# A hybrid RG-LRU / gated DeltaNet / attention backbone in fp32: four moves at the entry of the delta net

## What is computed

```python
q, k, v = jnp.split(jax.nn.silu(dw_conv(qkv, dn_cw)), [...], axis=-1)
q = l2_normalize(q.reshape(bsz, L, DN_HEADS, DN_DK)) * (DN_DK ** -0.5)
k = l2_normalize(k.reshape(bsz, L, DN_HEADS, DN_DK))
...
gcum = jnp.cumsum(to_chunks(g[..., None])[..., 0], axis=-1)
decay = jnp.exp(jnp.where(causal, gcum[..., :, None] - gcum[..., None, :], -jnp.inf))
m = jnp.where(strict, jnp.einsum('nbhid,nbhjd->nbhij', k_beta, kc) * decay, 0.0)
sol = lax.linalg.triangular_solve(eye + m, rhs, left_side=True, lower=True, unit_diagonal=True)
...
q_dec = qc * jnp.exp(gcum)[..., None]
```

## Time and profile before

| | |
|---|---|
| median of 3 runs | 1340.19 us |
| lowest, highest | 1338.09, 1348.91 us |
| the profiled execution, its own time | 1343.36 us |
| its span | 1341.6 us |
| TensorE busy | 1304.7 us (97%) |
| VectorE, ScalarE, GpSimd busy | 859.0 (64%), 681.5 (51%), 290.8 us (22%) |
| chain that ended last | TensorE 77%, VectorE 10%, ScalarE 5%, issue 3%, GpSimd 2%, DMA 1% |
| mean granted TensorE clock | 0.991 of full speed |

### The profile page before, as it was taken

One profiled execution on the slowest core, in us unless ns is written; L12 is line 12 of the kernel. 1 busy time (PEld: TensorE's weight loads), 2 busy tenths in 40 slices (PEclk: granted clock), 3 DMA queues, 4 the chain that ended last, 5 costly groups with the idle time before them and its releaser, 6 DMA issues.

```text
span 1341.6 us, 27229 instructions
## 1 busy us (share of the span) xinstructions
PE 1304.7 (97%) x10946; PEld 1226.9 (91%) x10946; DVE 859.0 (64%) x1271; ACT 681.5 (51%) x1098; POOL 290.8 (22%) x368
## 2 busy tenths in 40 slices
PE   6999999999799999999999999999999999999998
PEld 4899999997688888999999999999999988999998
DVE  4754789995457666533677656666736666875663
ACT  4458888866555554322534212343236665664553
POOL 3000223412587897513000000000130000200002
PEclk8999999999899999999999999999999999999999
DMA  9722323244231111123466566565423321556662
GB/s 325 209 80 81 94 79 95 80 114 151 98 111 33 49 48 33 64 95 110 146 202 196 181 193 195 183 197 178 129 95 126 97 69 32 182 173 220 190 201 80
DMA packets 138926, 174.90 MB, mean 130 GB/s; under 512 B 11025, under 2 KB 121873, under 8 KB 138561
## 3 DMA queue, kind: packets, MB, share of 16 engines
q1 hardware_dynamic: 137312, 168.94, 39.9%
q10 hardware_dynamic: 896, 4.23, 0.9%
q0 software_dynamic: 608, 0.19, 0.1%
HBM read 172.25 MB, written 1.08 MB: 129 GB/s over the span
## 4 chain that ended last, share of the span: by engine, by line
PE 77%; DVE 10%; ACT 5%; issue 3%; POOL 2%; DMA 1%; SPq 0%; ACTq 0%; DVEq 0%; POOLq 0%
PE bank L2728 54%; PE bank L2736 4%; DVE w_lo L1778 3%; DVE qkv L1864 2%; PE bank L3132 2%; PE bank L3141 2%; ACT w_hi L951 1%; PE bank L2654 1%; POOL qkv L806 1%; PE bank L3087 1%; PE bank L3408 1%; PE bank L3431 1%; DMA first_w<-in_w_mod 1%; PE bank L3006 1%; PE bank L3074 1%
## 5 line engine op out<-in xcount | busy, mean ns | idle before, releaser
L1778 DVE TENSOR_TENSOR w_lo<-raw,w_hi 128x1024 fp32r<-128x1024 f32 x212 | 264.2, 1247 | 297.1 <-ACT w_hi L951 296.6
L951 ACT ACTIVATE w_hi<-raw 128x1024 fp32r<-128x1024 f32 x212 | 223.9, 1057 | 379.9 <-PE bank L2728 371.8
L2728 PE MATMUL bank<-h_hi,w_hi 128*128 128x256 f32 x1472 | 299.4, 282 | 5.4 <-DVE w_lo L1778 2.9
L2728 PE MATMUL bank<-h_hi,w_lo 128*128 128x256 f32 x1472 | 293.7, 278 | 0.0
L2728 PE MATMUL bank<-h_lo,w_hi 128*128 128x256 f32 x1472 | 288.3, 278 | 0.0
L2728 PEld LDWEIGHTS bank<-h_hi,w_hi 128*128 128x128 f32 x1472 | 225.8, 189 | 15.5 <-issue 10.0
L2728 PEld LDWEIGHTS bank<-h_hi,w_lo 128*128 128x128 f32 x1472 | 225.7, 189 | 0.0
L2728 PEld LDWEIGHTS bank<-h_lo,w_hi 128*128 128x128 f32 x1472 | 222.6, 188 | 0.3 <-DVE h_lo L2076 0.2
L2728 PE MATMUL bank<-hid_hi,w_hi 128*128 128x256 f32 x768 | 172.0, 278 | 0.0
L2728 PE MATMUL bank<-hid_lo,w_hi 128*128 128x256 f32 x768 | 170.8, 277 | 0.0
L2728 PE MATMUL bank<-hid_hi,w_lo 128*128 128x256 f32 x768 | 170.7, 277 | 0.0
(11 more groups left out here) (380 smaller groups left out, 2445.3 us busy)
## 6 DMA issues: line engine op xcount, KB each, us to landing
raw<-in_mlp_w SPq DMA_DIRECT2D x128, 512.0 KB, 3.6
late_w<-in_w_mod SPq DMA_DIRECT2D x56, 512.0 KB, 4.4
raw<-in_even_w_in SPq DMA_DIRECT2D x48, 512.0 KB, 3.7
raw<-in_w_mod SPq DMA_DIRECT2D x24, 512.0 KB, 4.3
first_w<-in_w_mod SPq DMA_DIRECT2D x16, 512.0 KB, 11.2
raw<-in_even_w_out SPq DMA_DIRECT2D x16, 512.0 KB, 3.5
raw<-in_attn_w_qkv SPq DMA_DIRECT2D x16, 512.0 KB, 3.5
raw<-in_attn_w_o SPq DMA_DIRECT2D x8, 512.0 KB, 3.5
```

What stands on the lines that cost most here:

```text
L951: act.activation(stored(w_hi, j, four), raw[:, j % RAW], ACT.Copy).then_inc(hi_ready, 1)
L1778: dve.tensor_tensor(stored(w_lo, j, four), raw[:, j % RAW], stored(w_hi, j, four).bitcast(F32), ALU.subtract).then_inc(split_done, 1)
L2728: return pe.matmul(bank[2 * pair + t][:, c - n0:c - n0 + CTX], w_[:, k, t * P:(t + 1) * P], x_[:, c:c + CTX], start=(kk == 0 and first and ...
```

## The change

On VectorE the gate for b = 8's second pair goes from the end of b = 8 to behind `neighbours(0)` and `l2_scaled(1)` of b = 9, and the split of unit 6's weights behind it. On ScalarE the load of group 2 goes ahead of the roots of group 3, the table load ahead of the copies of near, and behind z the other table load and the two row readings come behind the two flipped copies. On TensorE the two row products of step 0 go from behind z to block 30 of z, into two banks, with waits of their own (reciprocal roots of groups 2 and 3); `decay(1)` goes ahead of `flip(0, 0, 0)` and waits for the first row reading (`a_row`); the wait behind z for the norms asks for group 2 only. On VectorE the split of unit 1 of segment out moves in step 0 from behind `scores(0)` to behind `neighbours(1)`.

```diff
--- before.py
+++ after.py
@@ -1172,10 +1172,10 @@
                     lru_gates(b, 1)
                 beside(b, 1)
                 if ends:
+                    act.preload_act_table_set("natural_log_exp_and_others")
                     neighbours(0)
-                    act.preload_act_table_set("natural_log_exp_and_others")
+                    l2_load(2)
                     l2_rstd(3)
-                    l2_load(2)
                 split_hi(u + 3, 3)
                 if b < LRU_TILES:
                     lru_tanh(b)
@@ -1421,7 +1420,7 @@
                 act.wait_ge(p_row, 2 * q + 2 - d)
                 if q >= 2:
                     act.wait_ge(p_os, q - 1)
-                act.activation(flat(d_qd[q % 2][:, d]), bank[R0][:, :], ACT.Exp).then_inc(a_row, 1)
+                act.activation(flat(d_qd[q % 2][:, d]), bank[R0 if q or d else R1][:, :], ACT.Exp).then_inc(a_row, 1)
 
             def flipped(q, l, c):
 
@@ -1469,10 +1468,11 @@
                 act.wait_ge(dnn["rs"], 2 * t + 1)
                 act.activation(y_, y_, ACT.Exp, scale=-0.5).then_inc(dnn["rs"], 1)
 
+            flipped(0, -1, 0)
+            flipped(0, -1, 1)
+            act.preload_act_table_set("natural_log_exp_and_others")
             rows(0, 1)
-            flipped(0, -1, 0)
             rows(0, 0)
-            flipped(0, -1, 1)
             for q in range(STEPS):
                 tail, prep = q >= 1, q + 1 < STEPS
                 gathered(q, 0, 0)
@@ -2000,8 +2000,9 @@
                     system(0)
                     for part in range(3):
                         neighbours(0, part)
+                    l2_scaled(1)
+                    evac(s, it - 1, 1)
                     split_lo(u + 2, 2)
-                    l2_scaled(1)
                 beside(b, 1)
                 split_lo(u + 3, 3)
                 if b == LRU_TILES:
@@ -2025,7 +2026,8 @@
                     masked(0, 0, 0)
                 if b == LRU_TILES - 1:
                     l2_squares(0, 1)
-                evac(s, it, 1)
+                if b != LRU_TILES:
+                    evac(s, it, 1)
 
             def act_base(name):
 
@@ -2385,13 +2387,13 @@
                 if prep:
                     neighbours(q + 1, 0)
                 scores(q)
-                if q == 0:
-                    split_lo(SEG["out"]["unit"] + 1, 1)
                 masked(q, 2, 0)
                 reduced(q, 1, 1)
                 if prep:
                     neighbours(q + 1, 1)
                     neighbours(q + 1, 2)
+                if q == 0:
+                    split_lo(SEG["out"]["unit"] + 1, 1)
                 if flip_turn(q):
                     evac_mod(flip_turn(q))
                 if tail:
@@ -3013,6 +3015,8 @@
                     pe.wait_ge(a_tok, 2 * q - 2)
                 elif q == 0:
                     pe.wait_ge(g_gate, 2)
+                else:
+                    pe.wait_ge(a_row, 1)
                 for d in range(2):
                     for g_ in (d_gu, d_gl):
                         mm = pe.matmul(bank[R0 if q else R2][:, :], lines[:, d], flat(g_[:, d]),
@@ -3021,14 +3025,16 @@
 
             def rows(q, d):
 
-                if d == 0:
+                if q == 0:
+                    pe.wait_ge(l2["rs"], 4 - d)
+                elif d == 0:
                     pe.wait_ge(a_row, 2 * q + 1)
                 elif q >= 3:
                     pe.wait_ge(dnn["rs"], 2 * (q - 3) + 1)
-                elif q:
+                else:
                     pe.wait_ge(a_near, 2 * q + 2)
                 for g_ in (d_gu, d_gl):
-                    mm = pe.matmul(bank[R0][:, :], lines[:, 2], flat(g_[:, d]), start=g_ is d_gu, stop=g_ is d_gl)
+                    mm = pe.matmul(bank[R0 if q or d else R1][:, :], lines[:, 2], flat(g_[:, d]), start=g_ is d_gu, stop=g_ is d_gl)
                 mm.then_inc(p_row, 1)
 
             def k_k(q):
@@ -3178,6 +3184,9 @@
 
                 def behind(k):
                     g = SUMS_BEHIND.get(UNIT_K * n + k)
+                    if UNIT_K * n + k == 30:
+                        rows(0, 1)
+                        rows(0, 0)
                     if g is None:
                         return
                     if g == 0:
@@ -3206,7 +3215,7 @@
                         gate_tokens()
 
             pe.wait_ge(l2["rs"], 4)
-            pe.wait_ge(l2["out"], L2_OUT[3])
+            pe.wait_ge(l2["out"], L2_OUT[2])
             pe.wait_ge(act_evac, 14)
             pe.wait_ge(a_vs, 24 - BY_POOL)
             def output_sum(t):
@@ -3223,9 +3232,7 @@
                 pe.matmul(bank[R0][:, :], C("ones"), norm_bufs(t)[0], start=True, stop=True).then_inc(dnn["ss"], 1)
 
             first_product(0, 0, 0)
-            rows(0, 1)
             flip(0, -1, 0)
-            rows(0, 0)
             for q in range(STEPS):
                 tail, prep = q >= 1, q + 1 < STEPS
                 t = q - 1
@@ -3237,15 +3244,13 @@
                     flip(0, -1, 1)
                     first_product(0, 0, 1)
                 mod_filler(mods_in(q, 0))
-                if prep and q:
+                if prep:
                     decay(q + 1)
                 if tail:
                     k_state(t, 0)
                 flip(q, 0, 0)
                 second_product(q, 0, 1)
                 mod_filler(mods_in(q, 1))
-                if prep and q == 0:
-                    decay(1)
                 if prep:
                     k_k(q + 1)
                 if tail:
```

## The result

Over 20 runs each the kernel before has a median of 1344.80 us, the changed one 1337.99 us; the ratio is 0.995, 95% interval 0.9936 to 0.9963, a gain of 5.0 to 8.6 us. The profiled execution of the changed kernel took 1337.51 us, its span 1335.7. The forecast was 6.7 us and 1333.5; the gain was met, and the measured median lies 4.5 above the forecast one because the first three executions of the kernel before (median 1340.19) were low for it. Two executions were far slower than all others of their kernel (1360.75 us of after_again, 1858.00 of lean_fillers) and are left out of every median and ratio here.

What follows compares the result with a forecast made beforehand. TensorE was taken as full from step 2 on, waits and low clock bounding the entry around z's end. 6.2 + 1.2 = 7.4 us, less 0.7 for clock, gives 6.7 us: median 1333.5 us, range 1329.5 to 1339.5.

Steps and rivals of the forecast that it cites:

- part 6: Step 0, VectorE: weight split behind the reduction to d_b shortens waits on d_pc and d_b, 1.2 us gain.
- part 5: Behind z, TensorE: decay(1) ahead of the flip; k_k(1) starts 6.2 us earlier, a figure that holds parts 1 to 4.
- Part 1: Within z: VectorE's gate behind l2_scaled(1) removes TensorE's 2.20 us wait; projection resumes 3.6 us earlier.
- Part 2: Row products inside z cost it 1.0 us, z ending at 336.9; they and a 2.4 us wait behind z go.
- Part 3: ScalarE: load of group 2 ahead of group 3's roots, issued at 321.2; d_t ends by 334.9, ahead of z's end.
- Part 4: ScalarE behind z: table change after the flipped copies, 1.28 us without a drain; betas(1) until 344.8, decay until 345.4.
- The clock: Entry behind z: TensorE's low clock at the remaining waits costs 0 to 1.5 us, 0.7 taken off the gain.
- (a): Rival: the wait moves to ScalarE's series behind z's last eviction, l2_scaled(3) late; gain 1 to 4.5, about 1337.5; chance 0.2.
- (b): Rival: row products only fill z, decay(1) gives waits back, steps 2 onwards take up the rest; 1340; chance 0.06.
- (c): Rival: slower, waits behind z keep TensorE at 1.2 GHz until k_k(2), up to 10 us more; 1343; chance 0.05.

Runs made afterwards that it cites:

- after_again: The changed kernel once more, no edit; 0.9954 of the kernel before.
- lean_fillers: The changed kernel with both the leaner entry and two filler units of step 0 moved into TensorE's wait; 1333.90 us, 0.9936 of the kernel before.
- before: The kernel without the change, the base of the ratios; median 1344.80 us over 20 runs.
- gate_alone: The kernel before with VectorE's gate moved and nothing else; 0.9988 of before.
- rows_back: The changed kernel with the two row products put back behind z, each in its own bank; one run, k_k(2) 58.26 us behind the sums of group 2.
- load_back: The changed kernel with the load of group 2 behind the roots of group 3 again; one execution, 1347.56 us.
- table_front: The changed kernel with ScalarE's table load and both row readings ahead of the two flipped copies; one run, k_k(2) 58.44 us behind the sums of group 2.
- before_again: The kernel before once more, no edit; k_k(2) starts 63.98 us behind the start of the sums of group 2, against 65.98.
- split_back: The changed kernel with the weight split back behind scores(0); 0.9976 of before.
- fillers_front: The changed kernel with two filler units of step 0 moved ahead of decay(1), into TensorE's wait; 0.9945 of before.
- lean_entry: The changed kernel with row products in banks R1 and R2, betas(1) ahead of z's last eviction, table load and row readings later; one run, 1332.68 us.
- after: The changed kernel as first traced; profiled execution 1337.51 us, median 1337.99 us, 0.995 of before.

## Why the prediction was right, step by step

The mechanism held, and the total within the noise. That the sum is met as well as it is, 6.7 against 6.8 us, is partly luck: z ended 1 us earlier than forecast, part 6 was priced too high, and part 5 was measured against one execution of before whose d_t ended 2.1 us later than in the other.

- **Part 1** (3.6 us): 3.4 to 3.9, all of it at the resume. The prediction gives it there and then one price, 6.2 us, for parts 1 to 5 together, which was right to do; what it does not say is that none of them carries alone. gate_alone shows 3.18 us of the gate's 3.9 as a wait behind z.
- **Part 2** (1.0 us for the products, z over at 336.9, that is 26.4 behind S): 0.93 us, and first_product at 25.25. The extra 1 us is from an earlier resume (0.3) and from the projection itself: the 120 matmuls took 13.9 us in place of 14.5. That the products had to go into z is not borne out (rows_back).
- **Part 3**: the times were right (load 321, l2_scaled(2) freed by siluz, d_t by 334.9; measured from S 1 us off at most), its meaning was not. "Ahead of z's end" is not the condition: d_tc and the table, 2.0 us, come between d_t and the eviction, and they ended 0.2 us behind z's end (1.4 in after_again). I gave the step no price; load_back puts it at 1.0 to 2.3 us at K1 and 3.0 to 3.9 at K2, the latter with clock and load waits in it. The end of d_t is what K1 follows in every execution of the changed kernel.
- **Part 4**: the series on ScalarE is as forecast, without a drain; that the flipped copies go ahead of the table is worth 0.8 us from d_tc to K1 and nothing at K2 (table_front).
- **Part 5** (K1 34.9 behind S; 6.2 us): 34.47 and 35.81. Against the two executions of before it is a gain of 3.0 to 6.7 us; from before_again alone, 3.0 to 4.3. Of the gain, 2.7 to 6.1 us are an earlier d_tc and 0.3 to 0.6 a shorter way from it to K1. TensorE's wait for a_row at decay(1) was 2.03 us ("about 2").
- **Part 6** (1.2 us): this term was too large. The wait of 1.2 us on d_pc went and that of 1.1 on d_b stayed, the foretold stall on the modulation load took 0.9 and 0.6 us, and with the split put back no loss is seen up to K2 that the clock does not account for (split_back).
- **The clock** (0.7 us lost of 0 to 1.5): it still falls behind z, 0.68 to 0.74 up to K1 in the two executions. fillers_front shows what was left in it: from d_tc to K2 1.8 to 2.1 us, the fillers' 1.0 us of moved work in it. It does not make the scatter at K1: from d_tc to K1 the changed kernel took 10.89 us at 0.74 and 11.00 at 0.68.
- **Rivals**: (a) named what bounds K1 behind d_t rightly, the series on ScalarE (lean_entry), and its single mishaps, low clock and the modulation stall, came; but l2_scaled(3) ended at 338.5 (26.6 behind S; (a) wanted 28.5); (b) and (c) did not happen. The "8 us of waits" held against (c) are 7.4 by the rows: 2.40, 0.64 and 2.56 in the three stretches and 1.79 ahead of them. That the steps behind are full is shown by every kernel here: matmul by matmul from K2 to 1000 us they agree with the changed kernel within 0.4 us, but for table_front, which won 1.1.

## What to carry to other kernels

Where several engines meet at one point, price the parts together: the gate alone was worth 1 to 3 us, the rest alone about nothing, all together 4 to 7. Here it took both tests, one part alone and one part put back, to see it. When a distance scatters between executions, look for the nearest instruction behind which it no longer does (here d_tc, behind which the changed kernel repeats within 0.1 us) before the clock is blamed. Ask of a moved wait what stands between its end and the point where it counts (here two copies and a table load), not only whether it ends before the other engine arrives. A short piece of work that is due later anyway can be worth more than its own time in a wait of TensorE, if it keeps the clock up: 1.8 to 2.1 us for 1.0 in fillers_front, in one execution. Where the wait was gone already it gained nothing (lean_fillers).

## What the runs showed of the hardware

TensorE's pace at full clock is not one number. The same 256-column matmuls, each with a weight load of its own, with no wait and a granted clock of 1.00, from 1200 to 1300 us in after and in split_back:

```profile
1200.00:1300.00 100.00, 100.00 (x885) 100.00 (x884) 62.75 (x85) 50.71 (x75) 2.95 (x3) 1.00 0.67 205
```

```profile
1200.00:1300.00 100.00, 100.00 (x851) 100.00 (x850) 61.40 (x84) 49.64 (x73) 0.00 (x0) 1.00 0.63 196
```

885 matmuls in 100 us are 113.0 ns each, 851 are 117.5. This 4% makes most of the 5.5 us by which split_back and load_back were longer behind K2 (4.2 of them by 1300 us). Within z it is part of before's 0.6 us; before_again's 0.6 goes with its clock, 0.70 for the first 2.2 us. The Trainium skill (TensorE: Matmul & The Clock Gate, Wait — 56ns, not 53.3ns?) gives N/2.4 + 2.5 ns from start to start back to back, by which 256 columns would take 109.2, an estimate; both paces here are slower. What chooses between them stays open; it was not tried. It may be one reason why the kernel before ran from 1338.09 to 1349.99 us in 20 runs.

GpSimd and VectorE slow each other, and here the first to start has the better of it. GpSimd's d_t took 2.48 us beside small instructions of VectorE. Beside VectorE's split and l2_scaled(3) it took 3.46 to 3.48 where it started first, and the split then 2.13 to 2.38 in place of 1.22; where the split started first, by as little as 0.07 us, it kept its 1.22 and d_t took 4.30 to 4.49. A lead of a tenth of a microsecond so decided 1.0 us on the way to K1 between after and after_again.
